# V projections moved beside the attention tasks of the pair ahead, FFN's ada rows behind its residuals, and the low parts of the head pairs on GpSimd

## Chip, cores and metric

The kernel runs on one core of a Trainium2 chip. The metric is the time of one launch on the device, in microseconds (us). Lower is better.

## What is computed

A streaming encoder trunk of two layers on a sequence of S = 1024 rows of D = 1024 values, in float32. The part that matters here is layer 0, "forgetting attention", and the ConvFFN of both layers:

```python
mod = c_act @ ada_w[l] + ada_b[l]              # shift, scale, gate rows, one dot product for each of 6*D
h = modulate(rmsnorm(x))
q, k, v, f = split(h @ w_in)                   # 16 heads of 64
F = cumsum(log_sigmoid(f + b_f))
p = softmax(q k^T / 8 + F_q - F_k, causal)     # per head
x = x + g1 * (concat_heads(p v) @ w_o)
h = modulate(rmsnorm(x))
x = x + g2 * ((silu(gate) * val) @ w_down)     # gate, val = causal conv(3) of h @ w_up
```

Layer 1 has windowed attention over a shared K/V and the same FFN. A final RMSNorm ends it.

## The kernel before

**Precision.** Each product of float32 operands is made as three products of a high part (rounded to fp32r) and a low part (the rest): high x high, high x low, low x high. So each operand is split first: a copy makes the high part, a subtraction the low part. `H` holds both parts of the modulated input, `w_spl` (3 slots) both parts of a weight tile, `w_raw` (2 slots) the tile as the SP queue loads it.

**The stream of weight tiles.** SP loads the tiles in the order of use. In the attention GpSimd splits each (`split`): it waits until the tile is loaded and until TensorE has let the slot go (`w_used`, counted up by TensorE at the first instruction after the last use of a tile), copies four quarters (L592) and subtracts four quarters (L599). GpSimd's program is in order, tile after tile.

**Attention of layer 0.** Four groups g of four heads. Each head has 12 tasks of 128 keys by up to 512 queries (`TASKS`, NT = 12), so T runs from 0 to 47 in a group and t is T modulo 12; a pair of heads is 24 tasks. For a task TensorE makes the scores (`score`: L918, L928, and L931 on the diagonal), ScalarE the exponential (`exp_task`, L1497) and its high part (`high_task`, L1504), VectorE the low part (`low_task`, L2090), and three tasks later (LAG = 3) TensorE multiplies by V (`value`, L953 to L955). Beside the tasks TensorE also makes, by tables of numbers: the row maxima of the next head (`maximum`, read on VectorE by L2064; then `turn_max` L902 transposes them, and `max_rows` L2082 on VectorE writes them into `QM`, for which the first `score` of the next head waits), and the Q and K projections of the pair ahead (`qk_step`, three matmuls of 512 columns a step).
The V projection of a whole group (`v_step`, 8 steps of 24 matmuls of 256 columns, with the columns of `H` as the stationary operand, so that V comes out with the keys on partitions) stands between two groups: steps 0 to 2 beside the last three tasks of a group, steps 3 to 7 by themselves with the maxima of the next head. `v_high` (ScalarE) and `v_low` (VectorE) split each step's result.

In the last group the output projection of the first seven pairs of heads is begun beside the tasks (`out_first`, at the tasks of `OUT_A_BESIDE`, six matmuls of 512 columns each). For it the pairs are loaded back from DRAM into `Hf` (which shares memory with H's low part), GpSimd makes the high part (L712) and VectorE the low part (`o_low`, L2118).

**FFN.** Pairs p of column tiles. From p = 2 (`NORMAL`) on, a pair is seven products (`seven`, Strassen) and half a down projection (`down`, four tiles m); a tile m may begin when VectorE has added the tile two before it to X (`half_residual`, L2285, counted by `dn_ev`). VectorE's program for a pair also has the sums of the seven products (`sum_of`), the taps of the convolution, and in layer 0 some ada rows (`step`, L1974: a dot product with a row that ScalarE's queue has loaded; a load waits until the step two before it has freed its buffer).

## Time and profile before

| | |
|---|---|
| median of 3 runs | 2390.47 us (2387.61 to 2393.91) |
| profiled execution | 2388.44 us, of which span 2386.6 us |
| busy share of the span | TensorE 96%, VectorE 65%, GpSimd 51%, ScalarE 48% |
| attention tasks of layer 0 | 115 to 609 us |
| FFN of layer 0 / layer 1 | about 700 to 1366 us / 1700 to 2373 us |

Times count from the start of the span. "Idle" is the time in which an engine ran nothing just before an instruction, and the name behind the arrow is what ended it. A matmul's duration holds the time in which it drains; the work that it takes from TensorE is the distance to the next start.

### The profile page before, as it was taken

The numbers are of one execution on the slowest core, as the hardware profiler recorded it, in microseconds if no ns is written. First come the engines' busy times: TensorE is split into PE (matmuls) and PEld (weight loads), VectorE is DVE, ScalarE is ACT, GpSimd is POOL, SyncE is SP. The second block draws the span as 40 slices with busy tenths as digits, with TensorE's granted clock in tenths as the row PEclk, the third lists the DMA queues.
The fourth block names the chain that finished last, engine by engine and source line by source line (L and its number), as shares of the span: only waits on it lengthen the run. The fifth ranks groups of instructions, "written<-read, shape, count | busy, mean of one in ns | idle before, by whom it ended". The sixth has DMA issues, their size and how long they took to land.

```text
span 2386.6 us, 30699 instructions
## 1 busy us (share of the span) xinstructions
PE 2293.8 (96%) x10986; PEld 1909.2 (80%) x10986; DVE 1541.0 (65%) x2536; ACT 1146.3 (48%) x1993; POOL 1209.4 (51%) x1641
## 2 busy tenths in 40 slices
PE   5999999998998999999999999989999999999998
PEld 4778788787877888888888878987778888888886
DVE  6565756658789677777776577882775555555556
ACT  5365664746255333333333496771553333333333
POOL 1501312133557666667666562214376666666663
PEclk9999999999999999999999999989999999999999
DMA  6211211114621333344332323233111111111112
GB/s 264 63 49 36 69 38 50 45 45 176 222 96 58 111 124 124 124 128 124 121 123 93 106 71 78 54 109 130 36 45 53 54 53 53 54 53 54 54 54 80
DMA packets 69082, 207.20 MB, mean 87 GB/s; under 512 B 7729, under 2 KB 8369, under 8 KB 68802
## 3 DMA queue, kind: packets, MB, share of 16 engines
q1 hardware_dynamic: 35248, 121.13, 15.7%
q10 hardware_dynamic: 33682, 84.11, 11.0%
q8 instruction: 87, 1.43, 0.2%
q14 instruction: 65, 0.53, 0.1%
HBM read 186.92 MB, written 16.32 MB: 85 GB/s over the span
## 4 chain that ended last, share of the span: by engine, by line
PE 80%; DVE 12%; ACT 4%; issue 2%; DMA 1%; SPq 0%; ACTq 0%; DVEq 0%
PE bank L1063 50%; PE bank L753 18%; PE bank L892 1%; PE bank L918 1%; PE bank L953 1%; PE bank L928 1%; PE bank L1280 1%; PE bank L955 1%; PE bank L954 1%; PE bank L1220 1%; DVE ada_raw L1974 1%; DMA ada_raw<-in_ada_t 1%; ACT H L1405 1%; DVE bank L2064 1%; DVE PL L2090 1%
## 5 line engine op out<-in xcount | busy, mean ns | idle before, releaser
L1063 PE MATMUL bank<-H,w_spl 128*128 128x512 f32 x3552 | 824.2, 390 | 8.2 <-DVE X L2285 6.5
L1063 PEld LDWEIGHTS bank<-H,w_spl 128*128 128x128 f32 x3552 | 667.6, 188 | 151.8 <-DVE X L2285 9.3
L651 POOL TENSOR_TENSOR w_spl<-w_raw,w_spl 128x256 fp32r<-128x256 f32 x688 | 551.3, 829 | 408.1 <-ACT w_spl L1647 406.7
L1063 PE MATMUL bank<-TB,w_spl 128*128 128x512 f32 x2112 | 493.6, 390 | 1.6 <-DVE TB L2245 1.6
L753 PE MATMUL bank<-H,w_spl 128*128 128x512 f32 x1920 | 481.3, 397 | 5.2 <-DVE H L2424 2.5
L1063 PEld LDWEIGHTS bank<-TB,w_spl 128*128 128x128 f32 x2112 | 396.1, 188 | 85.8 <-issue 3.4
L753 PEld LDWEIGHTS bank<-H,w_spl 128*128 128x128 f32 x1920 | 354.7, 190 | 76.2 <-DVE H L2424 2.9
L1647 ACT ACTIVATE w_spl<-w_raw 128x512 fp32r<-128x512 f32 x328 | 196.4, 624 | 348.0 <-PE bank L1063 291.8
L590 POOL TENSOR_TENSOR pace<-one_s 128x1 f32<-128x1 f32 x49 | 13.7, 280 | 578.9 <-PE bank L918 352.4
L2276 DVE TENSOR_TENSOR bank<-bank,sU 128x512 f32<-128x512 f32 x80 | 55.9, 699 | 280.7 <-PE bank L1063 280.7
L2285 DVE SCALAR_TENSOR_TENSOR X<-bank,mods,X 128x1024 f32<-128x1024 f32 x160 | 204.7, 1279 | 34.6 <-PE bank L1063 33.9
L599 POOL TENSOR_TENSOR w_spl<-w_raw,w_spl 128x256 fp32r<-128x256 f32 x200 | 170.8, 885 | 46.2 <-DVE H L1945 42.1
L658 POOL TENSOR_TENSOR w_raw<-w_raw 128x256 f32<-128x256 f32 x240 | 188.6, 806 | 9.4
L1662 ACT ACTIVATE sU<-bank 128x512 f32<-128x512 f32 x120 | 71.7, 598 | 245.9 <-PE bank L1063 205.4
L2064 DVE CUSTOM_DVE_ANT_0 bank<-bank,negF 128x128 f32<-128x128 f32 (+1 forms) x192 | 107.7, 568 | 98.4 <-PE bank L895 64.3
L1497 ACT ACTIVATE PF<-bank,negFT 128x512 f32<-128x512 f32 x192 | 110.9, 578 | 119.6 <-PE bank L931 86.8
L2090 DVE TENSOR_TENSOR PL<-PF,PH 128x512 fp32r<-128x512 f32 x192 | 111.9, 589 | 46.9 <-ACT PH L1504 45.2
L1504 ACT ACTIVATE PH<-PF 128x512 fp32r<-128x512 f32 x192 | 100.8, 525 | 6.1
L592 POOL TENSOR_SCALAR w_spl<-w_raw 128x256 fp32r<-128x256 f32 x196 | 88.9, 479 | 0.0
L2253 DVE SCALAR_TENSOR_TENSOR cG<-bank,conv_s,cG 128x1023 f32<-128x1023 f32 x44 | 56.5, 1283 | 45.6 <-ACT cG L1672 45.6
L1672 ACT ACTIVATE cV<-bank,conv_s 128x1024 f32<-128x1024 f32 x44 | 53.2, 1208 | 61.9 <-DVE bank L2274 61.9
L1974 DVE CUSTOM_DVE_ANT_0 ada_raw_f<-ada_raw_f,cbF,mods_a 128x512 f32<-128x512 f32 x68 | 58.3, 859 | 33.4 <-DMA ada_raw_f<-in_ada_t 33.4
(203 smaller groups left out, 3367.7 us busy)
## 6 DMA issues: line engine op xcount, KB each, us to landing
w_raw<-in_w_stream SPq DMA_DIRECT2D x184, 512.0 KB, 3.7
ada_raw_f<-in_ada_t ACTq DMA_DIRECT2D x136, 256.0 KB, 2.9
ada_raw<-in_ada_t SPq DMA_DIRECT2D x8, 1024.0 KB, 18.8
negF<-scratch_f ACTq DMA_DIRECT2D x16, 512.0 KB, 3.8
ada_raw_o<-in_ada_t ACTq DMA_DIRECT2D x4, 2048.0 KB, 8.1
ada_raw_o<-in_ada_t ACTq DMA_DIRECT2D x4, 1536.0 KB, 8.0
Hf<-scratch_o ACTq DMA_DIRECT2D x9, 512.0 KB, 4.5
X<-in_x_t SPq DMA_DIRECT2D x4, 1024.0 KB, 11.7
```

The source lines that it names most:

```text
L592: last = pool.tensor_scalar(w_spl[:, u % SPL, 0, q:q + 256], w_raw[:, u % RAW, q:q + 256], 1.0, 1.0, ALU.mult, ALU.mult)
L599: last = pool.tensor_tensor(w_spl[:, u % SPL, 1, q:q + 256], w_raw[:, u % RAW, q:q + 256], w_spl[:, u % SPL, 0, q:q + 256].bitcast(F32), A ...
L651: last = pool.tensor_tensor(block_at(layer, b, 1, q, q + 256), src[:, q:q + 256], block_at(layer, b, 0, q, q + 256).bitcast(F32), ALU.subt ...
L658: last = pool.tensor_tensor(dst[:, q:q + 256], x[:, q:q + 256], y[:, q:q + 256], op)
L753: last = pe.matmul(dst, stat(k, a), mov(k, b), start=(k == 0 and a + b == 0), stop=(k == KT - 1 and a == 1))
L1063: last = pe.matmul(dst, block_at(layer, b, x, k * P, k * P + P), mov(y), start=(start and x + y == 0), stop=(stop and x == 1), skip_group_ ...
L1497: nc.scalar.activation(PF[n_task % NP][:, 0:n], bank(4 + n_task % 2, 0, n), ACT.Exp, bias=negFT[:, kb, h:h + 1]).then_inc(p_exp, 1)
L1504: nc.scalar.activation(PH[n_task % NP][:, 0:n], PF[n_task % NP][:, 0:n], ACT.Copy).then_inc(p_hi, 1)
L1647: nc.scalar.activation(block_at(layer, b, 0), src, ACT.Copy).then_inc(b_hi, 1)
L2064: V_.tensor_tensor_reduce(bank(c % 2, 0, n), bank(c % 2, 0, n), negF[:, h % 2, k0:k0 + n], 1.0, NEG, ALU.add, ALU.max, mx[h % 2][:, i + 4 ...
L2090: V_.tensor_tensor(PL[n_task % NP][:, 0:n], PF[n_task % NP][:, 0:n], PH[n_task % NP][:, 0:n].bitcast(F32), ALU.subtract).then_inc(p_lo, 1)
L2285: V_.scalar_tensor_tensor(X[:, m], pair(4 + 2 * (m % 2)), mods[:, gc + m:gc + m + 1], X[:, m], ALU.mult, ALU.add).then_inc(dn_ev, 1)
```

## The change

**V.** Weight tiles come pair by pair now: Q, K, V. The V projection of pair r = 2 to 7 is made beside tasks 14 to 21 of the pair before it, with the weights as the stationary operand: for each of four quarters of the sequence two steps of 12 matmuls of 256 columns. The result has the head dimension on partitions. So ScalarE copies it to `vt` one task later, TensorE transposes it back into the other half of the same PSUM bank two tasks later (`turn_v`, two transposes), and ScalarE and VectorE split it three tasks later. Two banks (6 and 7) take turns: the step that opens quarter qd waits until VectorE has read quarter qd - 2. The Q and K steps fill tasks 0 to 12 of every pair alike (`FILL`). The maxima of each group's first head stand beside tasks too.

**Head pairs.** GpSimd makes the low parts of seven pairs after each high part. The loads wait for the last V step instead of the last Q/K step, and the steps of `out_first` stand 3, 2 and 1 tasks later at first.

**FFN.** For p = NORMAL the first residual goes ahead of two sums and the second ahead of two taps; in layer 0 the four ada steps go behind the third residual and their loads (steps 2 and 3) to the end of ScalarE's part; for the next pair the first ada step goes behind the first sum.

```diff
-V_EARLY = 3
-V_TASK = 4 * NT - V_EARLY
-FILL_1 = [2] * 16
-FILL_2 = [0] * (2 * NT) + [1, 1, 1, 1, 1, 2] * 2 + [3, 2, 2, 2] * 2
+FILL = [3, 2, 2, 3, 2, 2, 2, 2, 2, 3, 3, 3, 3]
+V_TASK = 14
-OUT_A_BESIDE = {25: (0,), 28: (1,), 31: (2,), 34: (3,), 37: (4,), 40: (5,), 44: (6,)}
+OUT_A_BESIDE = {28: (0,), 30: (1,), 32: (2,), 34: (3,), 37: (4,), 40: (5,), 44: (6,)}
...
+def v_beside(g, T):
+    q, t = divmod(4 * NT * g + T, 2 * NT)
+    return [(q + 1, t - V_TASK)] if 0 <= t - V_TASK < 8 and 1 <= q < NH // 2 - 1 else []
+def v_quarter(g, T):
+    return [(r, i // 2) for r, i in v_beside(g, T) if i % 2]
...
 # SP, ahead of the loads of the head pairs
-                            sp.wait_ge(qk_ps, 8 * NG)
+                            sp.wait_ge(v_ps, 8 + 4 * (NH // 2 - 2))
 # GpSimd, for each of seven head pairs, behind the high part
+                pool.wait_ge(o_hi, pr + 1)
+                for q in range(0, S, 256):
+                    last = pool.tensor_tensor(H[:, pr, 1, q:q + 256], Hf[:, pr, 1, q:q + 256],
+                                              H[:, pr, 0, q:q + 256].bitcast(F32), ALU.subtract)
+                last.then_inc(o_lo, 1)
 # TensorE
+            def v_step(r, i):
+                qd = i // 2
+                if i == 0:
+                    pe.wait_ge(w_ready, 3 * r + 3)
+                if i in (0, 2):
+                    pe.wait_ge(qk_lo, 2 * (4 * r + 3 + qd))
+                elif i % 2 == 0:
+                    pe.wait_ge(v_lo, 8 + 4 * (r - 2) + qd - 1)
+                last = product(bank(6 + qd % 2, 0, 256), w_tile(3 * r + 2), h_cols(256 * qd, 256),
+                               range(4 * (i % 2), 4 * (i % 2) + 4))
+                if i % 2:
+                    last.then_inc(v_ps, 1)
+            def turn_v(r, qd):
+                pe.wait_ge(vt_copy, 4 * (r - 2) + qd + 1)
+                for j in range(2):
+                    last = pe.transpose(bank(6 + qd % 2, 256 + j * P, 256 + j * P + P), vt[:, j * P:j * P + P], id_f[:])
+                last.then_inc(vt_ps, 1)
...
-                if T == 0:
-                    first.then_inc(w_used, 2 if g else 1)
+                if T % (2 * NT) == 0 and g + T != 2 * NT:
+                    first.then_inc(w_used, 1)
...
+                    for r, qd in v_quarter(g, T - 2):
+                        turn_v(r, qd)
...
+                    for r, tt in v_beside(g, T):
+                        v_step(r, tt)
 # ScalarE, task T, behind exp_task, high_task and the Q/K copies
+                    for r, qd in v_quarter(g, T - 1):
+                        copy_vt(r, qd)
+                    for r, qd in v_quarter(g, T - 3):
+                        v_high(r, qd)
 # VectorE, task T, behind low_task, the maxima and the Q/K low parts
+                    for r, qd in v_quarter(g, T - 3):
+                        v_low(r, qd)
-                    if g == NG - 1 and T in HEADS_SPLITS:
-                        o_low(HEADS_SPLITS[T])
 # FFN, VectorE
-                    step(0)
+                    if p > NORMAL + 1:
+                        step(0)
                     if p > NORMAL:
                         sum_of(p, 1, 1, 0, ALU.add, sU)
+                    if p == NORMAL + 1:
+                        step(0)
...
                     if p == NORMAL:
-                        step(2)
-                        step(3)
+                        half_residual(p, 0)
...
-                    half_residual(p, 0)
+                    half_residual(p, int(p == NORMAL))
                     taps(p, 1, pair(2))
-                    half_residual(p, 1)
+                    if p > NORMAL:
+                        half_residual(p, 1)
                     step(6)
                     gated(p)
                     half_residual(p, 2)
+                    if p == NORMAL:
+                        for i in range(4):
+                            step(i)
```

**Where the rows move.** First TensorE in the second half of a pair. Before, this piece is the start of a V projection of a group (bank1 is banks 4 to 7, w_spl the weights; L892 and L895 are maxima, L953 to L955 the product with V):

```order
L753 MATMUL bank1<-w_spl_55,H_49 128x256 [waits qk_lo]
L753 MATMUL bank1<-w_spl_55,H_49 128x256 x23
...
L753 MATMUL bank1<-w_spl_55,H_49 128x256 [waits v_lo]
L753 MATMUL bank1<-w_spl_55,H_49 128x256 x23
L753 MATMUL bank1<-w_spl_55,H_49 128x256 [waits v_lo]
L753 MATMUL bank1<-w_spl_55,H_49 128x256 x5
```

Now this stands at tasks 17 and 18 of a pair (L930 and L940 are the scores, L965 to L967 the product with V, L877 the transposes, L904 the maxima, L764 the V step):

```order
L877 MATMUL bank1<-id_f_134,vt_80 128x128 [waits vt_copy]
L877 MATMUL bank1<-id_f_134,vt_80 128x128
L904 MATMUL bank0<-KS0_60,QS0_56 128x512 [waits s_read]
L764 MATMUL bank1<-H_49,w_spl_55 128x256 x12
L930 MATMUL bank1<-QS1_57,KS1_61 128x512 [waits p_exp]
L940 MATMUL bank1<-QM1_59,KL1_63 128x512
L965 MATMUL bank0<-PH3_69,V_64 128x128 [waits p_lo]
L966 MATMUL bank0<-PH3_69,V_64 128x128
L967 MATMUL bank0<-PL3_77,V_64 128x128
L904 MATMUL bank0<-KS0_60,QS0_56 128x512 [waits s_read] x2
L764 MATMUL bank1<-H_49,w_spl_55 128x256 [waits v_lo]
L764 MATMUL bank1<-H_49,w_spl_55 128x256 x11
```

A V step is half as long, has a task's scores ahead of it, and the step at task 18 (and the one at task 20) waits for `v_lo`.

Second, ScalarE in its part for the same task 18, after the change (PF and PH are the exponential and its high part, L1501 is `copy_vt` for quarter 1, L1507 `v_high` for quarter 0):

```order
L1519 ACTIVATE PF2_72<-bank1,negFT_151 128x512 [waits pv_ps,s_ps]
L1526 ACTIVATE PH2_68<-PF2_72 128x512 [waits p_exp]
L1501 ACTIVATE vt_80<-bank1 128x256 [waits vt_ps,v_ps]
L1507 ACTIVATE V_64<-bank1 128x2x2x64 [waits pv_ps,vt_ps]
```

Before, ScalarE's part for this task had only the first two:

```order
L1497 ACTIVATE PF2_72<-bank1,negFT_150 128x512 [waits pv_ps,s_ps]
L1504 ACTIVATE PH2_68<-PF2_72 128x512 [waits p_exp]
```

Both V instructions stand behind the exponential of the task whose scores TensorE has just made.

Third, GpSimd at the end of the attention, before (L590 to L599 split tile 26, the last one ahead of the head pairs; L712 are the high parts of the first pairs):

```order
L590 TENSOR_TENSOR pace_144<-one_s_143 128x1 [waits w_used,raw_in0]
L592 TENSOR_SCALAR w_spl_55<-w_raw_54 128x256 x4
L599 TENSOR_TENSOR w_spl_55<-w_raw_54,w_spl_55 128x256 [waits w_hi]
L599 TENSOR_TENSOR w_spl_55<-w_raw_54,w_spl_55 128x256 x3
L712 TENSOR_SCALAR H_49<-Hf_50 128x256 [waits o_in0]
L712 TENSOR_SCALAR H_49<-Hf_50 128x256 x3
L712 TENSOR_SCALAR H_49<-Hf_50 128x256 [waits o_in1]
```

and after:

```order
L596 TENSOR_TENSOR pace_145<-one_s_144 128x1 [waits w_used,raw_in0]
L598 TENSOR_SCALAR w_spl_55<-w_raw_54 128x256 x4
L605 TENSOR_TENSOR w_spl_55<-w_raw_54,w_spl_55 128x256 [waits w_hi]
L605 TENSOR_TENSOR w_spl_55<-w_raw_54,w_spl_55 128x256 x3
L718 TENSOR_SCALAR H_49<-Hf_50 128x256 [waits o_in0]
L718 TENSOR_SCALAR H_49<-Hf_50 128x256 x3
L722 TENSOR_TENSOR H_49<-Hf_50,H_49 128x256 [waits o_hi]
L722 TENSOR_TENSOR H_49<-Hf_50,H_49 128x256 x3
L718 TENSOR_SCALAR H_49<-Hf_50 128x256 [waits o_in1]
```

Four subtractions have come in behind the four copies of each pair. Tile 26 takes the slot of tile 23. Before, tile 23 was the last K tile; now it is the V tile of pair 7, which TensorE lets go at the first score of task 24 of the last group.

## Rows read from the trace of the kernel before

**Rows 1.** Waits of TensorE, 212 to 570 us: us in total, times, longest.
```profile
PE bank L892 <- DVE mx L2064: 5.6, 9, 1.0
PE bank L918 <- DVE QM L2082: 3.9, 3, 1.4
PE bank L902 <- DVE nmx L2076: 2.9, 6, 1.0
```

**Rows 2.** A stretch: length, busy us of each engine (instructions), granted clock, DMA.
```profile
567.60:609.20 41.60, 39.21 (x209) 33.16 (x210) 36.60 (x73) 30.35 (x57) 3.54 (x7) 1.00 0.35 133
```

**Rows 3.** Timeline, 283 to 285 us: start, us, engine, line, instruction, [idle before].
```profile
283.57 0.39 PE L928 MATMUL bank<-QM,KL 128*128 128x512 f32 x1
...
284.00 0.69 ACT L1497 ACTIVATE PF<-bank,negFT 128x512 f32<-128x512 f32 x1 [1.54 <-PE bank L928]
284.72 0.63 ACT L1504 ACTIVATE PH<-PF 128x512 fp32r<-128x512 f32 x1
```

**Rows 4.** A V copy (timeline), and groups of the page (busy, mean ns).
```profile
510.74 0.38 ACT L1486 ACTIVATE V<-bank 128x256 fp32r<-128x256 f32 x1 [2.77 <-PE bank L753]
...
L1662 ACT ACTIVATE sU<-bank 128x512 f32<-128x512 f32 x120 | 71.7, 598 | 245.9 <-PE bank L1063 205.4
...
L2276 DVE TENSOR_TENSOR bank<-bank,sU 128x512 f32<-128x512 f32 x80 | 55.9, 699 | 280.7 <-PE bank L1063 280.7
```

**Rows 5.** Timeline of TensorE: three waits, the last ahead of four transposes.
```profile
143.63 0.79 PE L918 MATMUL bank<-QS,KS 128*128 128x512 f32 x1 [1.96 <-DVE QM L2082]
...
1377.27 7.05 PE L1205 MATMUL bank<-H,w_spl 128*128 128x512 f32 x21 [1.93 <-DVE H L1962]
...
1599.37 0.65 PE L1267 MATMUL bank<-id_f,PB 128*128 128x128 f32 x4 [2.31 <-DVE PB L2460]
```

**Rows 6.** Stretches behind the first two of these waits, columns as in rows 2.
```profile
143.63:150.00 6.37, 6.37 (x27) 6.13 (x28) 3.29 (x10) 3.45 (x7) 0.00 (x0) 0.56 0.18 64
1377.27:1383.00 5.73, 5.67 (x17) 4.12 (x17) 5.73 (x7) 3.87 (x7) 5.44 (x6) 0.70 0.22 82
```

**Rows 7.** Timeline of TensorE in the last group: scores 24, 28, 45, the last product.
```profile
567.59 0.50 PE L918 MATMUL bank<-QS,KS 128*128 128x512 f32 x1 [1.43 <-DVE QM L2082]
...
574.14 0.39 PE L918 MATMUL bank<-QS,KS 128*128 128x512 f32 x1
...
603.62 0.33 PE L918 MATMUL bank<-QS,KS 128*128 128x384 f32 x1
...
608.89 0.28 PE L955 MATMUL bank<-PL,V 128*128 128x128 f32 x1
```

**Rows 8.** GpSimd: tile 26 and the high parts (timeline), and a group of the page.
```profile
551.96 0.19 POOL L590 TENSOR_TENSOR pace<-one_s 128x1 f32<-128x1 f32 x1 [16.14 <-PE bank L918]
...
556.95 12.65 POOL L712 TENSOR_SCALAR H<-Hf 128x256 fp32r<-128x256 f32 x24
...
L651 POOL TENSOR_TENSOR w_spl<-w_raw,w_spl 128x256 fp32r<-128x256 f32 x688 | 551.3, 829 | 408.1 <-ACT w_spl L1647 406.7
```

**Rows 9.** VectorE's low parts of head pairs, 500 to 625 us (busy, mean ns).
```profile
L2118 DVE TENSOR_TENSOR H<-Hf,H 128x1024 fp32r<-128x1024 f32 x7 | 8.5, 1221 | 0.0
```

**Rows 10.** FFN, layer 0: VectorE's first ada row (timeline).
```profile
760.68 1.21 DVE L1974 CUSTOM_DVE_ANT_0 ada_raw_f<-ada_raw_f,cbF,modb 128x512 f32<-128x512 f32 x1
```

**Rows 11.** FFN, layer 0: TensorE (timeline), and ada loads (KB each, us to landing).
```profile
761.39 5.73 PE L1063 MATMUL bank<-H,w_spl 128*128 128x512 f32 x24 [0.83 <-POOL w_spl L651]
772.23 13.55 PE L1063 MATMUL bank<-H,w_spl 128*128 128x512 f32 x48 [5.11 <-DVE X L2285]
...
791.06 2.88 PE L1063 MATMUL bank<-H,w_spl 128*128 128x512 f32 x12
...
ada_raw_f<-in_ada_t ACTq DMA_DIRECT2D x8, 256.0 KB, 3.9
```

**Rows 12.** FFN, layer 1: TensorE (timeline).
```profile
1772.48 3.01 PE L1063 MATMUL bank<-H,w_spl 128*128 128x512 f32 x12 [0.56 <-DVE X L2285]
1776.36 8.48 PE L1063 MATMUL bank<-H,w_spl 128*128 128x512 f32 x36 [0.87 <-DVE X L2285]
```

More of the change, by code:

```diff
@@ L205, in qk_pos @@
         return 2 + n % 2
-    return 6 * (pair // 2) + 4 * (pair % 2) + n % 4 // 2
+    return 3 * pair + (pair == 1) + n % 4 // 2
 def qk_steps(g, T):
-    if T < 2 * NT:
-        fill, done, first = (FILL_1, 0, 8 * g + 4) if g else (FILL_1_FIRST, PREFACE, 4)
-    elif g < NG - 1:
-        fill, done, first = FILL_2, 0, 8 * g + 8
-    else:
-        return []
-    if T >= len(fill):
-        return []
-    a = done + sum(fill[:T])
-    return [(first + i // KT, i % KT) for i in range(a, a + fill[T])]
+    r, t = 2 * g + T // (2 * NT) + 1, T % (2 * NT)
+    fill, done = (FILL, 0) if r > 1 else (FILL_FIRST, PREFACE)
+    if 2 * r >= NH or t >= len(fill):
+        return []
+    a = done + sum(fill[:t])
+    return [(4 * r + i // KT, i % KT) for i in range(a, a + fill[t])]
+def v_beside(g, T):
[3 more added lines that the diff above has]
+    return [(r, i // 2) for r, i in v_beside(g, T) if i % 2]
 def qk_done(g, T):
@@ L845, in _ @@
                 qk_step(2, k)
-            def v_step(g, tt, between=True):
-                if tt == 0:
-                    pe.wait_ge(w_ready, 6 * g + 4)
-                if tt < 2:
-                    pe.wait_ge(qk_lo, 2 * (8 * g + 3 + tt))
-                else:
-                    pe.wait_ge(v_lo, 8 * g + tt - 1)
-                maxima = list(maxima_at(MAX_V, tt)) if between else []
-                for k in range(KT):
-                    last = product(bank(6 + tt % 2, 0, 256), lambda k, a: H[:, k, a, tt * P:tt * P + P],
-                                   lambda k, b: w_spl[:, 2 - k // 4 * 2, b, (k % 4) * 256:(k % 4) * 256 + 256], [k])
-                    if k == KT - 1:
-                        last.then_inc(v_ps, 1)
-                    if maxima and k in MAX_K:
-                        maximum(4 * g, maxima.pop(0))
-                    if between and tt == 7 and k == 2:
-                        turn_max(4 * g)
+            def v_step(r, i):
[15 more added lines that the diff above has]
+                last.then_inc(vt_ps, 1)
             def maximum(h, c):
@@ L987, in _ @@
             for g in range(NG):
-                for tt in range(V_EARLY, 8) if g else ():
-                    v_step(g, tt)
-                    if tt < V_EARLY + LAG:
-                        value(g - 1, 4 * NT - LAG + tt - V_EARLY)
                 for T in range(4 * NT):
@@ L1544, in _ @@
             act.wait_ge(z_v, 2)
-            v_high(0, 0)
-            v_high(0, 1)
+            first_v_high(0)
+            first_v_high(1)
             act.wait_ge(z_v, 3)
@@ L1551, in _ @@
             for j in range(2, 8):
-                v_high(0, j)
+                first_v_high(j)
             for n in range(2):
@@ L1564, in _ @@
             for g in range(NG):
-                for tt in range(V_EARLY, 8) if g else ():
-                    if tt == V_EARLY:
-                        v_high(g, tt - 1)
-                    v_high(g, tt)
-                    if tt in (5, 6):
-                        (log_sums, inverse_sums)[tt - 5](8 * g - 1)
-                    if tt == 7:
-                        send_head(4 * g - 1)
                 for T in range(4 * NT):
@@ L1784, in ffn @@
                         next_high(p, 3)
+                    if p == NORMAL:
+                        load(0)
+                        load(1)
                 block_high(PAIRS - 1, 12)
@@ L2041, in _ @@
             for j in range(2, 8):
-                v_low(0, j)
+                first_v_low(j)
             def qk_low(n, e):
@@ L2508, in layout @@
     tiles = []
-    for g in range(NG):
-        pair = [stationary(wq, 2 * g), stationary(wk, 2 * g)]
-        tiles += pair + moving(wv, 256 * g) if g else moving(wv, 0) + pair
-        tiles += [stationary(wq, 2 * g + 1), stationary(wk, 2 * g + 1)]
+    tiles += moving(wv, 0)
+    for r in range(NH // 2):
+        tiles += [stationary(w, r) for w in ((wq, wk, wv) if r > 1 else (wq, wk))]
     tiles += [stationary(a["a_w_o"][0], m) for m in range(8)]
```

106 lines of the change are left out of this document (49 added, 57 removed).

## Prediction, made before the changed kernel ran

> **What bounds the kernel.** The busy shares put TensorE first (96%), so I read its waits next, for only they and its work can move. From 212 to 570 us, three groups of heads, it waits 12.4 us: 5.6 for the reading of maxima, 3.9 for the maxima's rows in QM, 2.9 for the negated maxima [rows 1]. The longest, 1.43 us, stands at a score that opens a pair, behind tasks without Q/K steps [rows 7]. In the last half group it works 39.2 of 41.6 us, at full clock although a wait of 1.43 stands just ahead [rows 2, 7]. In the FFN the one large wait is 5.11 us for the first residual [rows 11]. So an edit gains at most these waits, and every new wait on TensorE costs in full. Then I took the order of the instructions and asked for each new wait what TensorE has to do while the chain behind it runs.
>
> **V beside the tasks: what it removes.** The same 576 matmuls of 256 columns are made. They now stand at tasks 14 to 21 of each pair, where the waits of rows 1 are. Six pair boundaries stay: at a boundary VectorE still needs about 1.3 us from the transposed maxima to QM, against about 1.3 of TensorE's work (task 23 and two transposes); bounds 0 to 1.4 each, I take 0.6, and 0.2 for `turn_v` at task 23. 12.4 - 6 x 0.8 = **7.6 us gained**.
>
> **What it adds: transposes.** 48 of 128x128. Four take 0.65 with the drain of about 0.2, 0.11 each [rows 5]: **5.3 us**.
>
> **What it adds: a wait at tasks 18 and 20.** The step of task 18 opens quarter 2, in the bank of quarter 0, and waits for quarter 0's `v_low`. VectorE can make that only behind `v_high`, which ScalarE has in its part for task 18, and ScalarE is in order: first exponential and high part of task 18, which need the scores that TensorE made at the start of that very task. Counted from TensorE's being free of score 18: the exponential starts 0.2 later (the score's last matmul starts at 283.57, takes 0.23 of TensorE, and the exponential starts at 284.00), 0.72 to the high part [rows 3], 0.6 for it, 0.35 for `copy_vt` (0.38 busy), 0.6 for `v_high`, 0.7 for `v_low`, 0.1 for two hand-overs [rows 4]: 3.25 us. TensorE has meanwhile three products of 128 columns (0.3) and two maxima (0.5) at task 18, three of 512 (0.75) and two short maxima (0.4) at task 20. It waits 2.5 and 2.1 us. Steps 14 and 16 wait for Q/K parts made long before. Six pairs: **27.6 us**. Behind the waiting step stand the next scores, so nothing else fills the gap. Bounds: nothing, if ScalarE could be a task ahead, which its order forbids, and the whole 3.25 twelve times, 39 us.
>
> **And the clock.** Behind the waits of 1.96 and 1.93 us the granted clock is 0.56 for 6.4 us and 0.70 for 5.7 us, against 1.00 otherwise: it stands partly at 1.2 GHz and costs 2.8 and 1.7 us [rows 5, 6]. Behind 1.43 it stayed at 2.4 GHz [rows 7, 2]. I take the lower cost (the first of the two had another wait just ahead) for each wait at task 18 and half of it at task 20: 6 x 2.55 = **15.3 us**, between 0 and 12 x 2.8 = 34.
>
> **Low parts on GpSimd.** Tile 26 now waits for the V tile's slot, let go at score 24. Count from that score, at 567.59 before. GpSimd needs 0.6 to start, 5.0 for the tile (551.96 to 556.95), then for each head pair 4 x 0.53 and 4 x 0.83 [rows 8], 5.5, of which I take 5.3, as VectorE is less busy. So the pairs are ready at 10.9, 16.2, 21.5, 26.8, 32.1, 37.4 and 42.7. TensorE reaches task 28 after 6.55 less one output step of 1.4, and its out step at 6.3 [rows 7]: it waits 4.6 us for the first pair and about 1 us for most that follow. The last step starts at 42.7, takes 1.4, and 5.5 remain (603.62 to 609.1): 49.6 instead of 41.5. **8 us lost**, the clock's loss behind the first wait included, since later waits swallow it. Bounds: 5, with pairs at 4.8 (what tile 26's same eight instructions took without their start), and 11, with pairs at 5.7. VectorE's seven low parts (1.22 each [rows 9]) were hidden behind TensorE, so their removal gives nothing. The loads start at task 21 and land before tile 26 is done.
>
> The Trainium skill, GPSIMD Engine Reference, "Elementwise — side-by-side cycle accounting", has GpSimd 1.96 times slower than VectorE in a subtraction of two inputs. The rows have 3.3 against 1.22, 2.7 times. By the page a pair would be ready every 4.5 us and the loss would be 3; the sum goes by the rows.
>
> **FFN, layer 0.** TensorE reached tile m = 2 at 766.99 (24 matmuls from 761.39, 0.227 each) and waited until 772.23 [rows 11]. VectorE is free of the low parts at 760.68 [rows 10]; without two ada rows the sum, ScalarE's tap (1.2) and two taps (2.5) end at 765.2 and the residual at 766.5: no wait, and the second residual ends at 768.9, before 769.7. But the ada rows are late next: the first two at 774 to 775.5, and ScalarE, in order, stands at the loads of the third and fourth until then, each 3.9 us to land, so the fourth is done at 780.2. Only then does it load the next pair's rows and copy product 1, which product 4 waits for (TensorE 780.6, copy 781.5), and the load ahead of the copy of product 3 waits for the first of the new rows (785.4, copy 786.6). TensorE starts product 5 at 786.6 instead of 791.06: 4.5 gained, less 1.0 for a clock that falls behind a wait of 2.4. **3.5 us gained**; bounds 1 and 7.6 (5.11 and the 2.5 by which the 48 matmuls behind it exceed 11.05).
>
> **FFN, layer 1.** No ada rows: waits of 0.56 and 0.87 and the delay between them go; m = 3 starts at 1774.3 instead of 1776.36 [rows 12]. **2.0 us gained**, between 1.4 and 2.0.
>
> **Sum.** -7.6 + 5.3 + 27.6 + 15.3 + 8.0 - 3.5 - 2.0 = +43.1 us on the profiled execution's 2388.4, 2431.5. The median of the runs is 2.0 above that execution: **2433 us**.
>
> **Rivals.**
> *The clock holds.* The waits are there, but they cost no clock, as behind 1.43 us. For it: busy stretches of 3 to 4 us between them. Against: both waits over 1.9 in rows 5 and 6. 2433 - 15 = 2418, down to 2411 with GpSimd's loss at 5 and the FFN's gain at 7.6. Chance 0.28.
> *The V chain is hidden (no slower than before).* Place: tasks 18 and 20. If the step did not wait, because the chain is done when TensorE arrives, 42.9 us drop out: 2433 - 42.9 = 2390, no change; with both of those bounds 2383. It decides where chain and clock cost under 1.5 us a pair (9 in all). For it: the ScalarE rows of a task are only 1.3 us and it idles half of the time. Against: the idling ends with the score it waits for. Chance 0.12.
> *More waits than these.* ScalarE late for `turn_v` at every quarter, or a clock that stays low from task 18 to the boundary: 5 us a pair more, about 2460. For it: the V parts add 4 x 1 us a pair to ScalarE. Against: at tasks 17, 19 and 21 a V step of 1.4 us lies between copy and transpose. Chance 0.08.
> *Forecast.* Waits and clock: 0.52, 2420 to 2454.
>
> **Numbers.** Low end 2409: the clock rival with those bounds, and a little for the boundaries; high end 2455: clock 2.8 behind each wait (+18), GpSimd 11 (+3), FFN 1 (+2). About 0.18 is left out. A difference under 0.3%, 7 us, can't be told from none. Slower is the forecast, the clock rival and the third: 0.88. The hidden chain splits: same 0.08, faster 0.04.
>
> **What would show it.** Right: waits of TensorE for VectorE's V low part, 12 of 2 to 2.5 us; a granted clock well under 1.00 in tasks 18 to 21 of each pair; a pair lasting about 74 us where it was 67 (134 for two); no large waits for maxima behind task 14; a wait of over 4 us for H's low part at task 28 of the last group, named GpSimd; no wait of 5 us at the first residual but two smaller ones for ScalarE's copies a pair later. Wrong: a pair at 67 us or less, or the wait under 1 us. The step on which most hangs is the order on ScalarE, then what 2 us of waiting does to the clock.

## The result: 0.63% slower, less than predicted

| | before | after |
|---|---|---|
| median | 2390.47 us | 2405.61 us (2402.95 to 2406.08, 5 runs) |
| ratio | | 1.0063, 95% interval 1.0052 to 1.0074 |
| profiled execution / its span | 2388.44 / 2386.6 us | 2406.08 / 2403.9 us |

The direction was right, but the predicted 2433 us lies 27 us too high, and its range began above the result, at 2409. The term for V was far too large, while the last group and the FFN of layer 0 came out dearer than forecast.

First the waits of TensorE after the change, 212 to 580 us, in the columns of [rows 1]:

```profile
PE bank L764 <- DVE V L2045: 17.3, 12, 1.6
```

The waits for maxima have all gone, and twelve waits for V's low part stand in their place, 1.64 us at task 18 and 1.25 at task 20 of each pair. The chain behind the first of them, in the timeline at task 18 of the second pair (start, us, engine, line, instruction):

```profile
285.04 0.40 PE L930 MATMUL bank<-QS,KS 128*128 128x512 f32 x1
285.27 0.40 PE L940 MATMUL bank<-QM,KL 128*128 128x512 f32 x1
...
285.70 0.69 ACT L1519 ACTIVATE PF<-bank,negFT 128x512 f32<-128x512 f32 x1 [1.34 <-PE bank L940]
285.79 0.68 PE L904 MATMUL bank<-KS,QS 128*128 128x512 f32 x2
...
286.43 0.63 ACT L1526 ACTIVATE PH<-PF 128x512 fp32r<-128x512 f32 x1
...
286.96 0.36 ACT L1501 ACTIVATE vt<-bank 128x256 f32<-128x256 f32 x1
287.23 0.38 ACT L1507 ACTIVATE V<-bank 128x256 fp32r<-128x256 f32 x1
...
287.63 0.42 DVE L2045 TENSOR_TENSOR V<-bank,V 128x256 fp32r<-128x256 f32 x1
...
288.11 1.69 PE L764 MATMUL bank<-H,w_spl 128*128 128x256 f32 x12 [1.64 <-DVE V L2045]
```

The places are those of the prediction: exponential, high part, `copy_vt`, `v_high`, `v_low`, V step. The sizes are not. The V instructions have 256 columns and take 0.38 and 0.42 us; from TensorE's being free of the score (285.50) to the step are 2.61 us instead of 3.25. The clock in two stretches behind such waits, and in the whole second half of the last group (columns as in [rows 2]):

```profile
288.11:294.00 5.89, 5.89 (x40) 5.40 (x41) 1.53 (x4) 2.42 (x4) 0.00 (x0) 1.00 0.22 47
...
588.00:594.00 6.00, 6.00 (x23) 4.94 (x24) 1.77 (x4) 2.36 (x4) 5.83 (x13) 0.73 0.89 365
...
576.49:629.05 52.56, 42.19 (x207) 35.04 (x208) 32.95 (x68) 30.56 (x58) 42.05 (x65) 0.94 0.45 167
```

Behind 1.64 us the clock stays at 2.4 GHz (1.00); behind the 5.02 us at task 28 it is partly at 1.2 GHz (0.73). The last line answers to [rows 2]: 41.6 us have become 52.6. GpSimd's timeline there, and what TensorE waited for in the last group:

```profile
577.14 0.34 POOL L596 TENSOR_TENSOR pace<-one_s 128x1 f32<-128x1 f32 x1 [25.19 <-PE bank L930]
...
582.86 2.09 POOL L718 TENSOR_SCALAR H<-Hf 128x256 fp32r<-128x256 f32 x4
585.03 2.77 POOL L722 TENSOR_TENSOR H<-Hf,H 128x256 fp32r<-128x256 f32 x4
587.77 1.51 POOL L718 TENSOR_SCALAR H<-Hf 128x256 fp32r<-128x256 f32 x4
589.37 2.81 POOL L722 TENSOR_TENSOR H<-Hf,H 128x256 fp32r<-128x256 f32 x4
```

```profile
587.95 2.90 PE L764 MATMUL bank<-H,w_spl 128*128 128x512 f32 x6 [5.02 <-POOL H L722]
...
603.27 1.65 PE L764 MATMUL bank<-H,w_spl 128*128 128x512 f32 x6 [1.24 <-POOL H L722]
...
615.53 2.93 PE L764 MATMUL bank<-H,w_spl 128*128 128x512 f32 x6 [3.30 <-POOL H L722]
```

Tile 26 starts 0.65 us after the score of task 24 (576.49), and the first pair is ready 11.3 us after it, close to the forecast (10.9). The sixth, for which TensorE waits 3.30 us, is ready at 39.0 us instead of 37.4. Its two rows on GpSimd, and two stretches as long as a low part, the second pair's and this one's (columns as in [rows 2]; the third busy time is VectorE's):

```profile
607.79 3.29 POOL L718 TENSOR_SCALAR H<-Hf 128x256 fp32r<-128x256 f32 x4
611.17 4.31 POOL L722 TENSOR_TENSOR H<-Hf,H 128x256 fp32r<-128x256 f32 x4
```

```profile
589.37:592.18 2.81, 2.81 (x11) 2.31 (x10) 0.01 (x1) 0.61 (x1) 2.81 (x5) 0.67 1.03 423
611.17:615.48 4.31, 1.06 (x6) 0.66 (x4) 4.21 (x6) 2.76 (x5) 4.31 (x5) 0.96 0.01 2
```

The same four subtractions of GpSimd took 2.81 us while VectorE ran for 0.01 us, and 4.31 while it ran for 4.21. The seven low parts of this trace follow that order: 2.77 to 2.88 us with VectorE busy for at most 0.54, 3.63 to 4.31 with it busy for 3.5 us or more. That is read off the trace; no run tests it as a cause.

The FFN of layer 0, timeline of TensorE (answers to [rows 11]):

```profile
780.78 16.62 PE L1075 MATMUL bank<-H,w_spl 128*128 128x512 f32 x72 [0.83 <-POOL w_spl L657]
...
802.09 4.57 PE L1075 MATMUL bank<-TB,w_spl 128*128 128x512 f32 x12 [1.98 <-ACT sU L1678]
...
809.61 4.58 PE L1075 MATMUL bank<-H,w_spl 128*128 128x512 f32 x12 [2.94 <-ACT s L1678]
```

The wait of 5.11 us has gone, and two for ScalarE's copies have come, each with slow matmuls behind it: twelve take 4.57 us instead of 2.88. (The granted clock in these two groups is 0.63 and 0.61.) In layer 1 both waits of [rows 12] are gone:

```profile
1785.55 16.62 PE L1075 MATMUL bank<-H,w_spl 128*128 128x512 f32 x72 [0.83 <-POOL w_spl L657]
```

Where the 17.3 us of the span lie, after less before, by the starts of the same instructions:

| stretch | us | predicted |
|---|---|---|
| up to the first task | +1.9 | 0 |
| six pairs with V (402.84 to 409.93) | +7.1 | +40.6 |
| second half of the last group, to its last product | +11.3 | +8.0 |
| from there to the FFN | -0.8 | 0 |
| FFN layer 0, first Strassen pair and start of the next | +0.85 | -3.5 |
| from there to the FFN of layer 1 | -0.9 | 0 |
| FFN layer 1 | -2.1 | -2.0 |

The first line is scatter between executions: FFN-only, below, has the code of before up to the FFN and starts its first task at 115.39 us, and the changed kernel with the heads on VectorE at 113.31.

### The profile page after: what moved, and what is told of

Same layout as the page of the kernel before. It is cut to its first block, busy times and chain, and to the rows that moved or that the text cites. A ratio compares the mean times of both kernels' runs of the same rounds, so it can differ in the third digit from the quotient of the medians.

```text
span 2403.9 us, 30907 instructions
## 1 busy us (share of the span) xinstructions
PE 2301.8 (96%) x11034; PEld 1917.7 (80%) x11034; DVE 1534.8 (64%) x2529; ACT 1152.8 (48%) x2017; POOL 1236.3 (51%) x1669
## 4 chain that ended last, share of the span: by engine, by line
PE 79%; DVE 12%; ACT 3%; DMA 2%; POOL 2%; issue 1%; ACTq 0%; SPq 0%; DVEq 0%; POOLq 0%
PE bank L1075 49%; PE bank L764 17%; PE bank L904 1%; PE bank L965 1%; PE bank L930 1%; PE bank L940 1%; PE bank L966 1%; PE bank L967 1%; PE bank L1292 1%; DVE ada_raw_o L1989 1%; PE bank L1232 1%; DVE bank L2085 1%; DMA ada_raw_o<-in_ada_t 1%; POOL H L722 1%; DVE ada_raw L1989 1%
## 5 line engine op out<-in xcount | busy, mean ns | idle before, releaser
L1075 PE MATMUL bank<-H,w_spl 128*128 128x512 f32 x3552 | 822.2, 390 | 4.6 <-ACT s L1678 2.9
L1075 PEld LDWEIGHTS bank<-H,w_spl 128*128 128x128 f32 x3552 | 667.4, 188 | 146.6 <-issue 3.4
L764 PE MATMUL bank<-H,w_spl 128*128 128x512 f32 (+1 forms) x2496 | 558.7, 373 | 32.2 <-DVE V L2045 17.3
L764 PEld LDWEIGHTS bank<-H,w_spl 128*128 128x128 f32 x2496 | 429.7, 190 | 110.8 <-DVE V L2045 21.2
L2111 DVE TENSOR_TENSOR PL<-PF,PH 128x512 fp32r<-128x512 f32 x192 | 117.4, 618 | 31.5 <-ACT PH L1526 30.0
L1989 DVE CUSTOM_DVE_ANT_0 ada_raw_f<-ada_raw_f,cbF,mods_a 128x512 f32<-128x512 f32 x68 | 58.9, 871 | 31.5 <-DMA ada_raw_f<-in_ada_t 31.5
## 6 DMA issues: line engine op xcount, KB each, us to landing
ada_raw<-in_ada_t SPq DMA_DIRECT2D x8, 1024.0 KB, 18.8
ada_raw_o<-in_ada_t ACTq DMA_DIRECT2D x4, 2048.0 KB, 10.9
```

The source lines that it names most:

```text
L764: last = pe.matmul(dst, stat(k, a), mov(k, b), start=(k == 0 and a + b == 0), stop=(k == KT - 1 and a == 1))
L1075: last = pe.matmul(dst, block_at(layer, b, x, k * P, k * P + P), mov(y), start=(start and x + y == 0), stop=(stop and x == 1), skip_group_ ...
L1989: V_.tensor_tensor_reduce(raw, raw, cb, 1.0, begin, ALU.mult, ALU.add, col).then_inc(ada_step, 1)
L2111: V_.tensor_tensor(PL[n_task % NP][:, 0:n], PF[n_task % NP][:, 0:n], PH[n_task % NP][:, 0:n].bitcast(F32), ALU.subtract).then_inc(p_lo, 1)
```

## Experiments

Ratios are to the kernel before, run on the same chip beside each; a difference in us between two kernels is the difference of their ratios times 2390.5.

**V's split one task earlier (`v_early`).**

```diff
 # ScalarE
-                    for r, qd in v_quarter(g, T - 3):
+                    for r, qd in v_quarter(g, T - 2):
                         v_high(r, qd)
 # VectorE
-                    for r, qd in v_quarter(g, T - 3):
+                    for r, qd in v_quarter(g, T - 2):
                         v_low(r, qd)
```

> The changed kernel, with ScalarE's high part and VectorE's low part of each V quarter placed one task earlier (task 17 instead of 18 and so on); nothing else moves. Theory 1 (the order on ScalarE makes the waits at tasks 18 and 20: the V high part stands behind the exponential of the very task in which TensorE waits): the waits of 1.64 and 1.25 us go, with about 0.15 us of drain each, 6 x 3.2 = 19 us less than the changed kernel, so about 2386 us, and a pair takes 65.1 us instead of 68.33. Rival (the waits only move: the quarter's low part now delays VectorE's reading of the maxima or the low parts of the probabilities): 5 us less or nothing, with new TensorE waits for VectorE's maxima or PL in tasks 17 to 23.

2383.95 us, 0.9979 (0.9970 to 0.9988): 20 us less than the changed kernel and 0.2% less than the kernel before. The waits of TensorE in its trace, 160 to 780 us, first lines:

```profile
PE bank L764 <- POOL H L722: 9.0, 4, 4.8
PE bank L930 <- DVE QM L2103: 4.0, 7, 1.3
```

No wait for V is left. A pair takes 65.28 us instead of 68.33, so the twelve waits with their draining and refilling cost 18.3 us. That is net: a wait of 0.44 to 0.46 us for QM comes back at each boundary, which the changed kernel did not show; VectorE could catch up there during the waits for V. Theory 1 holds: the order made the waits. The edit moves the parts of both engines; that ScalarE's place is the one that counts is seen in the changed kernel's timeline, where `v_low` starts 0.02 us after `v_high` ends (287.61).

**A longer V chain (`chain`, `chain_q0`, `chain_q1`).** The prediction had assumed waits of 2.5 and 2.1 us. Here such waits are made on purpose, first in quarters 0 and 1, then in one of them alone (`qd == 0`, `qd == 1`):

```diff
 # ScalarE, v_high
+                if qd < 2:
+                    nc.scalar.activation(spare[:], bank(6 + qd % 2, 256, HALF), ACT.Copy)
 # VectorE, v_low
+                if qd < 2:
+                    V_.tensor_tensor(spare[:].rearrange("p (t e d) -> p t e d", t=2, e=2),
+                                     bank(6 + qd % 2, 256, HALF).rearrange("p (t e d) -> p t e d", t=2, e=2),
+                                     V[:, 2 * qd:2 * qd + 2, r % 2, 0:3:2, :].bitcast(F32), ALU.subtract)
```

> The changed kernel, with one more ScalarE copy and one more VectorE subtraction of the same 128x256 (into a spare tile, used by nobody) ahead of the high part and of the low part of quarters 0 and 1 of each pair. They lengthen the chain that TensorE waits for at tasks 18 and 20 by about 0.4 + 0.4 us, to waits of about 2.4 and 2.05 us, which is what the prediction had assumed. Both theories have 12 x 0.8 = 9.6 us more for the waits. Theory 1 (the prediction's clock term: behind waits of about 2 us the granted clock falls, only the waits were shorter here than predicted): a further 6 x 2.55 = 15 us, +25 us in all, 2431 us, and a granted clock of 0.6 to 0.8 in tasks 18 to 21. Rival (the clock holds in these tasks whatever the wait): +9.6 us, 2415 us, with the granted clock at 1.00.

> The kernel with the longer V chain, with the extra ScalarE copy and VectorE subtraction for quarter 0 alone: waits of 2.25 us at task 18 and 1.25 us at task 20 of each pair, 6 x 0.6 = 3.7 us more than the changed kernel. There the clock fell behind two of the six waits of 2.25 us and behind all six of 1.85 us. Theory 1 (what decides is how idle the tasks around both waits are, so that one long wait is half as likely to bring the clock down): falls in some pairs, +4 to +10 us in all. Rival (each wait over 1.9 us brings it down by itself, as the prediction had it): six falls, +3.7 and 6 x 1.7 = +14 us. Second rival (only the second, shorter wait matters): no falls, +3.7 us, 2409 us.

> The same for quarter 1 alone: waits of 1.64 us at task 18 and 1.85 us at task 20, again 3.7 us more of waiting. Theory 1 (the two waits count together): falls in some pairs, +4 to +10 us. Rival (a wait of 1.85 us is what brings the clock down, whatever stands ahead): six falls, +14 us. Second rival (1.85 us is under the bound and the falls came from the 2.25 ahead of it): no falls, +3.7 us, 2409 us.

2425.3 us, 1.0149 (1.0133 to 1.0164); 2412.39 us, 1.0087 (1.0072 to 1.0103); 2420.06 us, 1.0121 (1.0104 to 1.0138). So +20.6, +5.7 and +13.9 us on the changed kernel, of which the longer waits alone are 7.3, 3.7 and 3.7. Timeline of TensorE in `chain`, three of the twelve waits:

```profile
219.74 1.70 PE L765 MATMUL bank<-H,w_spl 128*128 128x256 f32 x12 [2.25 <-DVE V L2052]
...
228.05 2.02 PE L765 MATMUL bank<-H,w_spl 128*128 128x256 f32 x12 [1.85 <-DVE V L2052]
...
290.84 2.93 PE L765 MATMUL bank<-H,w_spl 128*128 128x256 f32 x12 [2.25 <-DVE V L2052]
```

The same step behind the same wait takes 1.70 us once and 2.93 another time. The first stretch below is the one behind the first wait, the second begins 1.8 us after the end of the second wait, the last is the one behind the third:

```profile
219.74:225.00 5.26, 5.26 (x37) 4.91 (x38) 1.54 (x4) 1.84 (x3) 0.00 (x0) 1.00 0.22 50
229.87:232.80 2.93, 2.93 (x11) 2.49 (x11) 0.00 (x0) 1.10 (x2) 0.00 (x0) 0.53 0.00 0
290.84:294.30 3.46, 3.46 (x15) 3.32 (x16) 0.54 (x1) 0.00 (x0) 0.00 (x0) 0.53 0.00 0
```

A granted clock of 0.53 is close to the lower level, 1.2 GHz, for about three us. In `chain_q0` a pair takes 68.95 us where the clock held and 70.24 to 70.50 where it fell, so a fall costs 1.3 to 1.5 us. How often it fell in the one profiled execution of each (a fall shows in the length of the V step or of the score behind it, and makes the distance to the next such wait 1.3 to 1.6 us longer):

| kernel | wait at task 18: falls | wait at task 20: falls |
|---|---|---|
| changed | 1.64 us: 0 of 6 | 1.25 us: 0 of 6 |
| `turn2` (below) | 1.64 us: 2 of 6 | 1.25 us: 0 of 6 |
| `chain_q1` | 1.64 us: 2 of 6 | 1.85 us: 4 of 6 |
| `chain_q0` | 2.25 us: 3 of 6 | 1.25 us: 0 of 6 |
| `chain` | 2.25 us: 2 of 6 | 1.85 us: 6 of 6 |

So the prediction's clock term existed for the waits that it assumed (13.3 us measured in `chain` against 15.3), but neither theory is right: no length of one wait decides. 2.25 us brought the clock down less often than 1.85 us, which comes two tasks later in the pair. What decides it is left open; 1.25 us did it in none of 18 cases.

**Transposes twice (`turn2`).**

```diff
-                for j in range(2):
+                for j in (0, 1, 0, 1):
                     last = pe.transpose(bank(6 + qd % 2, 256 + j * P, 256 + j * P + P), vt[:, j * P:j * P + P], id_f[:])
```

> The changed kernel, with each of the 48 transposes of V made twice (the same result). Theory 1 (a transpose costs 0.11 us of TensorE, as the prediction has it): +5.3 us if all lie on the path. In tasks 17 and 19 the next wait for V's low part takes up part of it (the chain behind the wait starts at the following score, so it does not), so 2411 us. Rival (the 0.27 to 0.38 us that the trace shows for one or two transposes is their cost): +10 us or more. Second rival: hidden behind the waits, under 2 us.

2412.7 us, 1.0092 (1.0079 to 1.0106), +6.9 us. By the time alone theory 1 would pass, a little dear. The trace splits it otherwise (timeline, task 18 of pairs two to five):

```profile
289.48 1.70 PE L764 MATMUL bank<-H,w_spl 128*128 128x256 f32 x12 [1.64 <-DVE V L2045]
...
358.47 1.69 PE L764 MATMUL bank<-H,w_spl 128*128 128x256 f32 x12 [1.64 <-DVE V L2045]
...
427.46 2.58 PE L764 MATMUL bank<-H,w_spl 128*128 128x256 f32 x12 [1.64 <-DVE V L2045]
...
497.97 1.69 PE L764 MATMUL bank<-H,w_spl 128*128 128x256 f32 x12 [1.64 <-DVE V L2045]
```

Undisturbed pairs take 68.99 us, 0.66 more for eight more transposes: 0.08 each, 4.0 us for 48. The rest is two falls of the clock (the step of 2.58 us; the pair from it on takes 70.51).

**Head pairs' low parts on VectorE (`heads_vec`), and the V slot let go earlier (`slot`).**

```diff
 # heads_vec: the subtraction of GpSimd is left out, and VectorE has at the end of its part for a task
+HEADS_SPLITS = {28: 0, 29: 1, 31: 2, 33: 3, 36: 4, 39: 5, 42: 6}
+                    if g == NG - 1 and T in HEADS_SPLITS:
+                        o_low(HEADS_SPLITS[T])
 # slot, in TensorE's score
-                if T % (2 * NT) == 0 and g + T != 2 * NT:
+                if g + T == 0 or T % (2 * NT) == 22 and 1 <= 2 * g + T // (2 * NT) <= NH // 2 - 2:
                     first.then_inc(w_used, 1)
```

> The changed kernel, with the low parts of the seven head pairs back on VectorE (1.22 us each, at tasks 28, 29, 31, 33, 36, 39 and 42 of the last group); GpSimd makes the high parts alone, 2.1 us each behind tile 26. Theory 1 (GpSimd's pace makes the waits at the later head pairs, tile 26's late slot makes most of the first): the first wait of 5.0 us falls to about 3.7, those of 1.24 and 3.30 us go, and the slow clock behind the last one goes too (about 1.4 us): 7 us less, 2398.5 us. Rival (the split of tile 26 alone sets the last half group): about 1.5 us less, 2404 us. Second rival (VectorE is now late for the low parts of the probabilities): no gain, new waits of TensorE for PL.

> The changed kernel, with the V tile's slot let go at the score of task 22 of its pair, right behind the last V product, instead of at the first score of the next pair. Theory 1 (tile 26's slot, then GpSimd's pace, sets the second half of the last group): in the changed kernel these scores lie at 573.79 and 576.49 us, so tile 26, the seven head pairs and the waits behind them come 2.7 us earlier: the first wait 2.3 instead of 5.0 us, the end of the group 2.7 us earlier, 2403 us. Rival 1 (the loads of the head rows, 6.5 us each from task 21 on, are then what the first pair waits for): about 1 us earlier only. Rival 2: less than 1 us in all, since GpSimd's later pairs have other waits.

`heads_vec` 2396.75 us, 1.0029 (1.0018 to 1.0041), 8 us less; `slot` 2403.29 us, 1.0056 (1.0043 to 1.0069), which the times alone don't tell from the changed kernel. The first head pairs in the timelines, `heads_vec` (two waits) and then `slot`:

```profile
583.59 2.90 PE L760 MATMUL bank<-H,w_spl 128*128 128x512 f32 x6 [3.14 <-DVE H L2135]
...
591.52 1.96 PE L760 MATMUL bank<-H,w_spl 128*128 128x512 f32 x6 [1.62 <-DVE H L2135]
```

```profile
583.96 1.61 PE L764 MATMUL bank<-H,w_spl 128*128 128x512 f32 x6 [2.48 <-POOL H L722]
...
611.27 2.93 PE L764 MATMUL bank<-H,w_spl 128*128 128x512 f32 x6 [3.31 <-POOL H L722]
```

From the score of task 24 to the last product (41.3 us before, 52.6 after) these profiled executions take 50.0 and 50.3 us. `slot` halves the first wait, but the last, 3.31 us, stays: GpSimd's pace makes that one. `heads_vec` takes out the pace, but not tile 26, and TensorE now waits for VectorE's low parts (two more waits, 0.73 and 0.22 us). Its trace has only 2.6 us of the 8 that its times have; the profiled execution took 2400.59 us, 3.8 above the median, with the clock down behind both of the waits shown (0.50 and 0.63 in the 4.4 us behind them). Other runs may have fewer falls, which no trace shows.

**The FFN part alone (`ffn_only`), and two ada rows back in their places (`res_mid`).** `ffn_only` is the kernel before with the diff's FFN part. `res_mid` is the changed kernel with:

```diff
 # VectorE, p = NORMAL: steps 0 and 1 ahead of the first residual again, 2 and 3 stay behind the third
-                    if p > NORMAL + 1:
+                    if p != NORMAL + 1:
                         step(0)
...
-                    if p > NORMAL:
-                        step(1)
+                    step(1)
+                    if p > NORMAL:
                         step(2)
...
-                        for i in range(4):
-                            step(i)
+                        step(2)
+                        step(3)
 # ScalarE, p = NORMAL: load(0) and load(1) around tap(p, 0) again instead of at the end
```

> The kernel before with only the change's FFN part (ada rows behind the residuals of the first Strassen pair, on VectorE and ScalarE). By the trace of the changed kernel: layer 0 +0.85 us (the wait of 5.11 us gone, two of 1.98 and 2.94 for ScalarE's copies in its place, each with a slow clock behind it), layer 1 -2.1 us, sum -1.2 us, 2389 us. The prediction had -5.5 us for it, 2385 us. Rival: the V layout or the clock's history ahead of the FFN made the two waits, so that by itself the edit gains the 5.5 us.

> The changed kernel, with the first two ada rows of the first Strassen pair and the loads of the third and fourth back at their places of before (ahead of the residual, about 1.5 us of VectorE); the first residual stays ahead of the third and fourth row. Theory 1 (ScalarE, in order, is held at the loads of the third and fourth ada row until VectorE has done the first two, and so comes late with the copies of the next pair): the waits of 1.98 and 2.94 us for ScalarE's copies and the slow clock behind them go, a wait of about 1.2 us at the first residual comes back: 5 us less, 2400.5 us. Rival (the copies are late for the other ada rows, which are still made behind the residuals): one of the two waits stays, 2 us less or nothing.

`ffn_only` 2387.78 us, 0.9986 (0.9977 to 0.9995), 3.3 us less than before; `res_mid` 2402.06 us, 1.0052 (1.0038 to 1.0065), 2.6 us less than the changed kernel. From the first output tile of p = 2 to the same product later `ffn_only` takes 32.38 us (before 32.39), the changed kernel 33.24 and `res_mid` 28.56. So the edit of layer 0 gives nothing by itself, and its gain lies in the ada rows' places. (This stretch of `res_mid` is 4.7 us shorter than the changed kernel's, close to the 5 expected; its times have 2.6, with intervals that allow either.) The rival of `ffn_only`, that the layout of V or the clock's history made the two waits, fails: with the attention of before, both are there, and only the second has a slow clock behind it:

```profile
784.11 2.97 PE L1063 MATMUL bank<-TB,w_spl 128*128 128x512 f32 x12 [1.02 <-ACT sU L1662]
790.87 5.45 PE L1063 MATMUL bank<-H,w_spl 128*128 128x512 f32 x12 [3.79 <-ACT s L1662]
```

ScalarE in the changed kernel (timeline; ACTq is its queue's own issue of loads):

```profile
789.11 1.14 ACT L1663 ACTIVATE w_spl<-w_raw 128x512 fp32r<-128x512 f32 x2
794.71 1.01 ACTq L1720 DMA_DIRECT2D ada_raw_f<-in_ada_t  x2
795.82 1.16 ACT L1663 ACTIVATE w_spl<-w_raw 128x512 fp32r<-128x512 f32 x2 [5.57 <-DVE mods_a L1989]
799.74 0.33 ACTq L1718 DMA_DIRECT2D cbF<-scratch_c  x1
800.10 1.15 ACTq L1720 DMA_DIRECT2D ada_raw_f<-in_ada_t  x2
801.35 0.60 ACT L1678 ACTIVATE sU<-bank 128x512 f32<-128x512 f32 x1 [4.38 <-issue]
...
807.91 0.34 ACTq L1720 DMA_DIRECT2D ada_raw_f<-in_ada_t  x1
808.35 0.63 ACT L1663 ACTIVATE w_spl<-w_raw 128x512 fp32r<-128x512 f32 x1 [5.88 <-DVE mods L1989]
...
808.88 0.58 ACT L1678 ACTIVATE s<-bank 128x512 f32<-128x512 f32 x1
```

ScalarE stands at each load until VectorE has made the ada rows (L1989), and the copies that TensorE waits for stand behind it: theory 1. In `res_mid` TensorE has one wait instead, for the first residual:

```profile
787.63 12.80 PE L1075 MATMUL bank<-H,w_spl 128*128 128x512 f32 x48 [2.03 <-DVE X L2290]
```

**All four (`best`), and better places (`best2`).** `best` has the edits of `v_early`, `heads_vec` (head pair 0 at task 27), `slot` and `res_mid`. `best2` is `best` with:

```diff
-HEADS_SPLITS = {27: 0, 29: 1, 31: 2, 33: 3, 36: 4, 39: 5, 42: 6}
+HEADS_SPLITS = {27: 0, 28: 1, 30: 2, 32: 3, 35: 4, 38: 5, 41: 6}
-OUT_A_BESIDE = {28: (0,), 30: (1,), 32: (2,), 34: (3,), 37: (4,), 40: (5,), 44: (6,)}
+OUT_A_BESIDE = {29: (0,), 31: (1,), 33: (2,), 35: (3,), 38: (4,), 41: (5,), 45: (6,)}
```

> The changed kernel with four edits at once: the V high and low parts one task earlier, the head pairs' low parts on VectorE (the first at task 27), the V tile's slot let go at task 22, and the first two ada rows at their places of before. If the four causes are separate, their gains add: 2405.6 - 21.7 (measured) - 8.9 (measured) - 2.7 - 5 = about 2367 us, 1% under the kernel before. Rival (they overlap: with the waits for V gone VectorE has less time, and the low parts of the heads and the maxima compete for it): 2375 us or more, with new waits for VectorE in the last group.

> The kernel with four edits at once, with the first half product's steps of the output projection one task later (29, 31, 33, 35, 38, 41, 45) and VectorE's low parts of head pairs 1 to 6 one task earlier (28, 30, 32, 35, 38, 41). Theory 1 (its waits of 0.80, 1.81 and 0.76 us for VectorE's low parts of the heads come from their places in the program, behind maxima and the division of O): they go, with the slow clock behind the second, 4 us less, 2370.5 us. Rival (the low parts then delay the maxima or the low parts of the probabilities by as much): no change.

`best` 2374.59 us, 0.9938 (0.9925 to 0.9950); `best2` 2371.75 us, 0.9917 (0.9903 to 0.9932), 0.8% faster than the kernel before. The second half of the last group takes 45.0 us in `best` and 41.1 in `best2`, as short as before (41.3; 42.8 in `ffn_only`, which has the same code there). `best` is 8 us above its expected 2367, of which the two smaller gains, measured at 1.7 and 2.6 us where 2.7 and 5 were expected, explain 3.4, and the two larger, 20.1 and 8.1 by the ratios where 21.7 and 8.9 were put in, 2.4. By the measured ratios alone the sum would be 0.9927, inside the interval of `best`. But what the rival named is there too: new waits for VectorE in the last group, of 0.80, 1.81, 0.76 and 0.22 us for the heads' low parts, the second at task 30:

```profile
570.84 2.93 PE L760 MATMUL bank<-H,w_spl 128*128 128x512 f32 x6 [1.81 <-DVE H L2136]
```

In `best2` they have gone; one of 1.23 us for VectorE's `O_st` and one of 0.48 for a maximum have come. The two profiled executions as a whole are equally long (2374.48 and 2375.02 us), since that of `best2` reaches its first pair with V 3.5 us later, ahead of anything that `best2` changes; the gain of 3.9 us is that of the last group.

## Why the prediction was too high

The sum had 43.1 us, the traces have 17.3. Of the 25.8 us between them the clock term is 15.3 too much, the waits at tasks 18 and 20 are 9.3 too much, and the removed waits together with the transposes gain 8.8 more than forecast. The last group (3.3) and the FFN of layer 0 (4.35) went the other way.

**V, the wait at tasks 18 and 20 (27.6 us): place right, size wrong.** Number (twelve), tasks, chain and cause were as forecast, and `v_early` shows that the order on ScalarE is the cause. It cost 18.3 us net of the QM waits that it hides. The failed step is the sizing of `v_high` and `v_low`: 0.6 and 0.7 us came from 128x512 instructions of the FFN [rows 4], though the instructions have 256 columns, and the row of a 128x256 V copy, 0.38 us, stood in the same group. In order, an instruction also starts before the one ahead has ended: `v_high` starts 0.27 us after `copy_vt`, which has 0.36 busy.

**The clock (15.3 us): it did not come.** The term rested on waits of 2.1 to 2.5 us. At 1.64 and 1.25 us there was no fall in the six pairs of the profiled execution. `chain` shows 13.3 us where the waits are 2.25 and 1.85, so the sum was about right for the waits assumed, in part by luck: it had the full cost at task 18 and half of it at task 20, and the falls came 2 and 6 of 6 times. As a rule for every wait near 2 us it was wrong. The rival "the clock holds" named this, but kept the waits at their predicted size.

**Removed waits (7.6 us gained) and transposes (5.3 lost).** In the changed kernel all waits for maxima went; with the chain mended, 6 x 0.45 us come back where 6 x 0.8 were forecast. A transpose costs 0.08 us (`turn2`), 4.0 in all. `v_early`'s pairs are 11.1 us shorter than those of before, where these two terms as predicted give 2.3: here the failed step is a gain sized too small. In numbers of the traces: the six pairs took 402.84 us before, of them 14.2 waits, and take 391.72 in `v_early`, of them 2.7 waits. So the waits fell by 11.5 us, and all else grew by 0.4 (388.6 to 389.0), although the transposes alone are 4.0 of it. Other work gave back about 3.6: the 576 V products, summed from start to start, take 70.2 us instead of 71.4 (waits not counted), and most of the rest lies at the places of the 18 waits that went, which cost TensorE its draining and a slower first matmul besides their idle time (behind a wait a score of 512 columns holds it 0.34 us instead of 0.23). This split was only read off, no run tests it. The prediction left out waits of other kinds (1.8 us for KL and for the scores' issue) and what a wait costs besides its idle time.

**Low parts on GpSimd (8 us, bound 11): it cost 11.3.** First pair, place and name were right. For most later pairs it had waits of about 1 us each; there were two waits, of 1.24 and 3.30 us. The slow clock behind the first wait (0.73) was swallowed by these, as forecast. The failed step is GpSimd's even pace of 5.3 us a pair. On average it held (5.34), but the sixth pair took 7.65, with VectorE busy in 7.2 of them, and was ready 1.6 us late. Behind the wait for it the clock stood at 0.75 for 6 us, the output step took 2.93 us instead of 1.6, and no later wait swallowed that: the last step started 45.95 us behind score 24, where 42.7 was forecast. Two causes overlap. Tile 26's slot or GpSimd's low parts taken out alone leave 50 us of the 52.6, the V waits taken out alone (`v_early`) 51.9; all of them together, with the tasks of the low parts and of the output steps chosen for it, bring 41.1. The first two without the third were not run. The Trainium skill, GPSIMD Engine Reference, "Elementwise — side-by-side cycle accounting", measured GpSimd 1.96 times slower than VectorE in an add of two inputs. The changed kernel has 2.77 us for the subtraction against 1.22 of [rows 9], 2.3 times, where VectorE stood idle beside it, and 4.31 us, 3.5 times, where it was busy; the sum used 2.7.

**FFN, layer 0 (3.5 us gained): 0.85 lost.** The prediction had the mechanism, ScalarE held at the loads until VectorE has done the ada rows, and its times hold up to the fourth row: 18.8 us behind the first output tile, in forecast (780.2 less 761.39) and trace (799.6 less 780.78). The failed step is what follows: the new pair's first row was to be done 24.0 us behind that tile, and ScalarE passed the load that waits for it only at 27.1 (807.9). The mis-sized term is the 3.9 us of a load: the three loads that ScalarE issued from 799.74 on, `cbF` and two ada rows, took 6.7 to 7.0 us to land, and VectorE stood waiting for them. The first copy was late for another reason, ScalarE's issuing of these three loads (799.74 to 801.25), for which the prediction left 0.7 us. So waits of 0.9 and 2.4 us became 1.98 and 2.94, and each had a slow clock behind it (1.7 us each, where 1.0 was taken for both). Layer 1, with no ada rows, came out at the forecast: 2.1 us for 2.0.
